# Expert blocks: down-projection weights in two fp32r halves, and two row buffers in place of three

## The reference, cut to what matters

```
def expert_block(args):
    tok, e = args
    xb = h_pad[tok]                                     # 128 gathered rows of 1024
    a = jax.nn.silu(xb @ w_gate[e]) * (xb @ w_up[e])    # 128 x 256
    return a @ w_down[e]                                # 128 x 1024
```

## Time and profile before

| what | value |
|---|---|
| median of 3 runs | 3767.45 us (3759.51 to 3767.55) |
| profiled execution, its time | 3764.93 us |
| its span | 3763.1 us |
| PE busy | 3462.2 us, 92% |
| DVE busy | 2725.4 us, 72% |
| ACT busy | 1236.3 us, 33% |
| POOL busy | 485.1 us, 13% |
| the two expert sections | from about 2012 to 2673 us, and 3047 to 3700 us |

### The profile page before, as it was taken

One profiled execution on the slowest core, in us unless ns is written; L12 is line 12 of the kernel. 1 busy time (PEld: TensorE's weight loads), 2 busy tenths in 40 slices (PEclk: granted clock), 3 DMA queues, 4 the chain that ended last, 5 costly groups with the idle time before them and its releaser, 6 DMA issues.

```text
span 3763.1 us, 51806 instructions
## 1 busy us (share of the span) xinstructions
PE 3462.2 (92%) x20788; PEld 2831.3 (75%) x20788; DVE 2725.4 (72%) x3133; ACT 1236.3 (33%) x1641; POOL 485.1 (13%) x465
## 2 busy tenths in 40 slices
PE   8998999999997999998889999999679789999995
PEld 8996798999984788996546776776567666776774
DVE  8877577879877577876667777777464677777774
ACT  1013111000024211011324565565221345655652
POOL 0000220101001210101001121221010011211210
PEclk9999989999998899999989999999899999999998
DMA  6545333454544333541026999999632269999993
GB/s 242 185 161 198 116 134 125 179 190 180 195 160 155 135 124 137 188 157 67 23 90 239 377 364 360 362 359 369 242 123 101 78 223 337 343 343 332 344 333 127
DMA packets 118803, 799.30 MB, mean 212 GB/s; under 512 B 33808, under 2 KB 34832, under 8 KB 48400
## 3 DMA queue, kind: packets, MB, share of 16 engines
q1 hardware_dynamic: 78480, 735.14, 52.6%
q0 software_dynamic: 39024, 59.61, 4.7%
q10 hardware_dynamic: 1040, 1.05, 0.1%
HBM read 808.77 MB, written 71.83 MB: 234 GB/s over the span
## 4 chain that ended last, share of the span: by engine, by line
PE 56%; DVE 9%; ACT 3%; issue 1%; DMA 1%; POOL 0%; DVEq 0%; ACTq 0%; SPq 0%; POOLq 0%
PE ps L433 52%; PE ps L447 4%; DVE ring_r L391 1%; DMA arena<-yd_dram 1%; DVE ring_r L390 1%; DVE arena L2050 1%; ACT arena L1689 0%; ACT arena L1871 0%; DMA ring<-stream_dram 0%; DVE ring_r L2557 0%; DVE arena L1855 0%; DVE mrow L1853 0%; ACT arena L1824 0%; ACT arena L1866 0%; DVE arena_r L516 0%
## 5 line engine op out<-in xcount | busy, mean ns | idle before, releaser
L433 PE MATMUL ps<-arena_r,ring_r 128*128 128x256 f32 (+1 forms) x9968 | 1301.6, 290 | 57.7 <-DVE ring_r L391 26.1
L433 PEld LDWEIGHTS ps<-arena_r,ring_r 128*128 128x128 f32 x9968 | 1249.8, 191 | 95.0 <-DVE ring_r L391 26.9
L433 PE MATMUL ps<-ring_r,arena_r 128*128 128x512 f32 (+1 forms) x2440 | 664.0, 388 | 6.0 <-DVE arena_r L1922 5.1
L433 PEld LDWEIGHTS ps<-ring_r,arena_r 128*128 128x128 f32 x2440 | 442.8, 189 | 97.2 <-DVE arena_r L1922 5.5
L433 PE MATMUL ps<-ring,arena 128*128 128x512 f32 (+1 forms) x1224 | 491.0, 544 | 1.0 <-DVE arena L2592 1.0
L391 DVE TENSOR_TENSOR ring_r<-ring,ring_r 128x4096 fp32r<-128x4096 f32 (+2 forms) x111 | 483.2, 4353 | 3.8
L2557 DVE TENSOR_TENSOR ring_r<-ring,arena_hi 128x2048 fp32r<-128x2048 f32 x154 | 353.1, 2293 | 98.8 <-ACT arena_hi L2602 88.1
L433 PE MATMUL ps<-arena_hi,arena_r 128*128 128x512 f32 x1232 | 406.4, 397 | 0.0
L433 PEld LDWEIGHTS ps<-ring,arena 128*128 128x128 f32 x1224 | 220.3, 192 | 197.5 <-issue 185.2
L433 PE MATMUL ps<-arena 128*128 128x128 f32 (+5 forms) x1728 | 252.4, 326 | 88.5 <-DMA arena<-yd_dram 32.7
L390 DVE CAST ring_r<-ring 128x4096 fp32r<-128x4096 f32 (+2 forms) x111 | 275.8, 2485 | 69.9 <-PE ps L433 57.5
(11 more groups left out here) (322 smaller groups left out, 3079.3 us busy)
## 6 DMA issues: line engine op xcount, KB each, us to landing
ring<-wexp_dram SPq DMA_DIRECT2D x387, 1024.0 KB
ring<-stream_dram SPq DMA_DIRECT2D x143, 2048.0 KB, 7.8
arena<-yd_dram SPq DMA_DIRECT2D x12, 2048.0 KB, 10.4
xd_dram<-arena POOLq DMA_DIRECT2D x6, 512.0 KB, 5.9
consts_sb<-consts_dram SPq DMA_DIRECT2D x1, 2242.0 KB, 16.1
arena<-xd_dram,small POOLq DMA_INDIRECT x129, 8.9
yd_dram<-arena,small POOLq DMA_INDIRECT x129, 8.2
arena<-mem_dram POOLq DMA_DIRECT2D x2, 1024.0 KB, 5.3
```

Source lines behind the costliest of these rows:

```text
L433: return pe.e.matmul(ps, lhsT=lhsT, rhs=rhs, start=start, stop=stop, skip_group_check=True)
```

## The change

The down weights of a block are handled as the gate and up weights are. ACT casts each 512-column half of them to a high half (`act_high_down`, two casts per block, behind silu); POOL, not DVE, subtracts for the low half (`low_down`, two subtractions per block), in place in the ring. `down` on PE becomes 12 fp32r matmuls. DVE now leaves two buffers for the hidden values, the cast `ATH` and the low half `ATL`. The room for the new high halves (three places of 1024 columns, `down_at`) comes from the third row buffer and from one of the five places of "a" and "b", which now rotate through four. POOL fetches three blocks ahead instead of four.

```diff
@@ places
-        for i, o in enumerate((4096, 6144, 8192 + 4096)):
+        for i, o in enumerate((4096, 6144, 8192 + 4096, 8192 + 10240)):
...
-        XB = [sub(8192 + 1024 * i, 1024) for i in range(3)]
+        XB = [sub(8192 + 1024 * i, 1024) for i in range(2)]
...
-                self.hi_at = [rings_r[:, 2048 * (NRAW + i):2048 * (NRAW + i) + 2048] for i in range(10 - NRAW)] + [h[:, :] for h in hi_parts]
+                self.hi_at = [rings_r[:, 2048 * (NRAW + i):2048 * (NRAW + i) + 2048] for i in range(10 - NRAW)] + [h[:, :] for h in hi_parts[:2]]
+                self.down_at = [hi_parts[2][:, 0:1024], hi_parts[2][:, 1024:2048], hi_parts[3][:, :]]
...
+            def raw_down(self, i, nn, of=rings):
+                return v3(self.raw("d", i, of), 1024)[:, :, 512 * nn:512 * nn + 512]
@@ pe_section, down
-                wd = S.raw("d", i)
+                ah, al = as_r(ATH.v()), as_r(ATL.v())
                 for nn in range(2):
                     ps = take(pe, K, "y", i, nn)
                     for k in range(2):
-                        o = 1024 * k + 512 * nn
+                        wh, wl = S.hi_down(i, nn)[:, k, :], S.raw_down(i, nn, rings_r)[:, k, :]
                         pe.wait_ge(*at("left", K, "h", i))
-                        pe.wait_ge(*S.got("d", i))
-                        ins = mm(pe, ps[:, :], AT.v(128 * k, 128), wd[:, o:o + 512], k == 0, k == 1)
+                        pe.wait_ge(*at(K, "split down", i, nn))
+                        mm(pe, ps[:, :], ah[:, col(k)], wh, k == 0, False)
+                        mm(pe, ps[:, :], ah[:, col(k)], wl, False, False)
+                        ins = mm(pe, ps[:, :], al[:, col(k)], wh, False, k == 1)
@@ dve_section
-                    dve.next.tensor_copy(AT.v(0, 256), bank(K, "h", i)[:, 0:256]).then_inc(*dve.mark("left", K, "h", i))
+                    ah, al = as_r(ATH.v()), as_r(ATL.v())
+                    dve.next.tensor_copy(ah, bank(K, "h", i)[:, 0:256]).then_inc(*dve.mark())
+                    dve.next.tensor_tensor(al, bank(K, "h", i)[:, 0:256], ah.bitcast(F32), ALU.subtract).then_inc(*dve.mark("left", K, "h", i))
@@ act_section
+        def act_high_down(act, S, i, nn):
+            act.wait_ge(*S.got("d", i))
+            old = 2 * i + nn - len(S.down_at)
+            if old >= 0:
+                act.wait_ge(*at("ps", S.key, "y", old // 2, old % 2))
+            act.next.copy(S.hi_down(i, nn), S.raw_down(i, nn)).then_inc(*act.mark(S.key, "high down", i, nn))
...
                     act.next.activation(SUM.v(0, 256), bank(K, "hidden", i)[:, 0:256], ACT.Silu, bias=0.0, scale=1.0).then_inc(*act.mark(K, "silu", i))
+                    act_high_down(act, S, i, 0)
+                    act_high_down(act, S, i, 1)
@@ pool_section
+            def low_down(i, nn):
+                pool.wait_ge(*at(K, "high down", i, nn))
+                pool.next.tensor_tensor(S.raw_down(i, nn, rings_r), S.raw_down(i, nn), S.hi_down(i, nn).bitcast(F32),
+                                        ALU.subtract).then_inc(*pool.mark(K, "split down", i, nn))
-            for i in range(min(4, n)):
+            for i in range(min(3, n)):
                 fetch(i)
             for i in range(n + 1):
-                if i + 1 < n and i + 4 < n:
-                    fetch(i + 4)
+                if i + 3 < n:
+                    fetch(i + 3)
+                if i < n:
+                    low_down(i, 0)
                 if i:
                     put(i - 1)
+                if i < n:
+                    low_down(i, 1)
```

More of the change, by code:

```diff
@@ L271, in build @@
         hi_parts = []
-        for i, o in enumerate((4096, 6144, 8192 + 4096)):
-            hi_parts.append(nc.alloc_sbuf_tensor_at(f"arena_hi{i}", [128, 2048], F32R, offset=arena_at + 4 * o))
+        for i, o in enumerate((4096, 6144, 8192 + 4096, 8192 + 10240)):
+            hi_parts.append(nc.alloc_sbuf_tensor_at(f"arena_hi{i}", [128, 2048 if i < 3 else 1024], F32R, offset=arena_at + 4 * o))
         out_parts = []
@@ L290, in build @@
                               [semaphore(f"sec_weights_{i}_{l}_{b0}") for i in range(NRAW)],
-                              [semaphore(f"sec_x_{i}_{l}_{b0}") for i in range(3)],
+                              [semaphore(f"sec_x_{i}_{l}_{b0}") for i in range(2)],
                               [semaphore(f"sec_y_{i}_{l}_{b0}") for i in range(2)])
@@ L2219, in build @@
         XH = [sub(6144 + 1024 * i, 1024) for i in range(2)]
-        SUM, AT = sub(15360, 512), sub(15872, 256)
+        SUM, ATH, ATL = sub(15360, 256), sub(15872, 256), sub(16128, 256)
         OH = [sub(512 * i, 512) for i in range(4)]
@@ L2467, in hi, with hi_down @@
                 return self.hi_at[(2 * i + (part == "b")) % len(self.hi_at)]
+            def raw_down(self, i, nn, of=rings):
+                return v3(self.raw("d", i, of), 1024)[:, :, 512 * nn:512 * nn + 512]
+            def hi_down(self, i, nn):
+                return v3(self.down_at[(2 * i + nn) % len(self.down_at)], 512)
             def got(self, part, i):
@@ L2474, in got_x @@
             def got_x(self, i):
-                return self.x[i % 3], 16 * (i // 3 + 1)
+                return self.x[i % 2], 16 * (i // 2 + 1)
             def put_y(self, i):
@@ L2489, in all_done @@
                     eng.wait_ge(*self.got(*it))
-                for i in range(max(0, self.n - 3), self.n):
+                for i in range(max(0, self.n - 2), self.n):
                     eng.wait_ge(*self.got_x(i))
@@ L2504, in turn @@
                         pe.wait_ge(*S.got_x(i))
-                        ins = tr(pe, ps[:, col(j)], XB[i % 3].v(512 * g + 128 * j, 128))
+                        ins = tr(pe, ps[:, col(j)], XB[i % 2].v(512 * g + 128 * j, 128))
                     ins.then_inc(*pe.mark("ps", K, "x", i, g))
@@ L2640, in fetch @@
             def fetch(i):
-                if i >= 3:
-                    pool.wait_ge(*at("ps", K, "x", i - 3, 1))
+                if i >= 2:
+                    pool.wait_ge(*at("ps", K, "x", i - 2, 1))
                 pool.e.indirect_dma_start(
-                    out=XB[i % 3].v(), out_offset=None, in_=xd,
+                    out=XB[i % 2].v(), out_offset=None, in_=xd,
                     in_offset=bass.IndirectOffsetOnAxis(ap=TOKEN_OF[:, S.b0 + i:S.b0 + i + 1], axis=0),
-                    bounds_check=128 * nt - 1, oob_is_err=False).then_inc(S.x[i % 3], 16)
+                    bounds_check=128 * nt - 1, oob_is_err=False).then_inc(S.x[i % 2], 16)
             def put(i):
```

## The result

| | before | after |
|---|---|---|
| time, median | 3767.5 us (3759.51 to 3767.56, 4 runs) | 3811.74 us (3811.39 to 3817.31, 4 runs) |
| ratio, 95% interval | | 1.013 (1.0116 to 1.0143) |
| profiled execution, time and span | 3764.93, 3763.1 us | 3811.55, 3809.7 us |
| one block, both sections | 10.07 us | 10.41 us in a regular turn |
| first to last output copy, sections 1 and 2 | 637.8, 627.8 us | 663.6, 654.4 us |

The kernel became 1.3% slower, 44 us by the medians, where the forecast of 3842 us had 77 us of loss. The direction and the mechanism came out, the size did not: a block takes 0.34 us longer than before, not 0.57. This block time is the round that POOL and DVE go through together.

What follows compares the result with a forecast made beforehand. PE was taken to bound the kernel, with transfers close behind. Ring 71 us, section ends 4 and starts 2 gave 77 us on the profiled 3764.93 us, so 3842 us; range 3765 to 3900.

Steps and rivals of the forecast that it cites:

- PE: Down on PE takes 2.83 us instead of 3.43, saving 0.60 us a block; PE alone would need 9.47 us.
- ACT and DVE's small parts: ACT's two casts, 2.2 us, fit in 2.45 us before the output copy; DVE's added subtraction, priced at 0.42, costs nothing.
- Room: Fewer row buffers and high places cost nothing in between; a gather is still issued almost two turns (20 us) ahead.
- The meeting: POOL's and DVE's subtractions with two SBUF operands do not run together; one stands still until the other is done.
- The signs that the forecast named: PE below 95%, DVE's subtractions 3.4 then 2.29 us, POOL's first 2.4 to 3.6, pitch near 10.6, transfers near 0.93.
- The ring: POOL's two subtractions, scatter and DVE's pair make a 10.64 us round, 0.57 above 10.07; 125 turns, 71 us.
- The missed turn: Rival: POOL's second subtraction is ready after 4.85 us, DVE goes first; 1.5 us more per block, 3960 us, chance 0.08.
- The ends: The last block of a section waits for both POOL subtractions: 1.9 us more per section, 4 us in all.
- the sections' starts: The third gather waits for the first block's transposes: 0 to 2 us per section, 1 taken, so 2 us.
- The transfers: Transfers limit a block to some 9.77 us (9.87 and 9.67 by layer), cutting off about half of PE's gain.
- the likeliest case: The forecast's own case, the ring of POOL and DVE: 3842 us, own range 3790 to 3885, chance 0.74.
- the first rival: No meeting of POOL and DVE: PE's gain arrives and transfers take over at 9.77 us, 3733 us, chance 0.12.

Runs made afterwards that it cites:

- e3_no_low: Changed kernel without POOL's two subtractions, the product with the low half using the high half again: 3706.33 us.
- e4_room: Kernel before with only the room taken away (two row buffers, gathers three blocks ahead, four high places): 3765.4 us, ratio 1.000.
- e2_memset: Changed kernel with POOL's subtractions replaced by memsets of about 2.5 us each, high half used in place of low: 3719.05 us.
- e6_copy: Changed kernel with each POOL subtraction replaced by two one-operand in-place copies, high half in place of low: 3748.41 us.
- e5_half: Changed kernel with halves for the first 512 down columns only, the other 512 plain float32 matmuls: 3724.7 us, ratio 0.9891.
- e8_three_of_four: Changed kernel with three of four 128 x 512 down-weight pieces in halves, the fourth plain float32: 3721.64 us, ratio 0.988.
- e1: Changed kernel with POOL's order changed, both subtractions of a block before the scatter: 3806.59 us, ratio 1.0112.
- e7: Changed kernel with the second subtraction of a block moved from POOL to DVE, before DVE's weight subtractions: 3752.73 us, ratio 0.9967.

## Why the prediction was right in kind and wrong in size

**PE.** Right. Down now takes twelve matmuls at a pitch of 0.229 us, 2.75 us (2.83 forecast), and without the low half a block of the second section takes 9.47 us (e3_no_low), the forecast's sum.

**ACT and DVE's small parts.** Right: the two casts of the down weights (2.19 us in the block shown) lie in front of the output copy, and neither they nor DVE's added subtraction are on the chain. ACT's share of the chain is its casts of rows and gate and up weights, which now lie inside the round.

**Room.** Right: it costs nothing (e4_room).

**The meeting.** Right. It is exclusion of POOL's reads of SBUF by DVE's two-operand subtraction and the reverse: DVE's instruction goes back to 2.29 us when POOL writes only (e2_memset), is late behind a one-operand copy (e6_copy), and is untouched where the slot suffices (e5_half, e8_three_of_four). The gather that begins inside the pair is held too: it takes 2.89 us and ends 0.9 us behind the first instruction of the pair; DVE's second instruction is not held by it. The signs that the forecast named came as well: PE at 92% of the stretches, the first of DVE's pair at 3.24 us, POOL's first subtraction at 3.5 to 3.6; only the pitch, 10.41, is below its 10.6.

**The ring.** This is the term that was mis-sized, not its form. Forecast: 2.22 + 0.31 + 1.01 + 0.2 + 2.36 + 4.54 = 10.64. Measured: 2.25 + 0.14 + 1.00 + 0.03 + 2.41 + 4.55 = 10.38. In order: POOL's first subtraction, a gap, the scatter, a gap, the second subtraction, DVE's pair. The four durations were right to 0.05 us each; the two gaps were 0.17 us too long each. I had taken the gap in front of the scatter from scatter to gather, a gap between two indirect DMAs, and put it where arithmetic comes before the DMA. In the timeline of after, DMA behind arithmetic waits 0.14 us, and arithmetic behind a DMA 0.03 us. As the ring is only as bad as it exceeds 10.07, an error of 2% in it was one of 40% in the loss: (10.64 - 10.41) x 125 = 29 us, beside the 30 us by which the forecast missed; the other errors nearly cancel (see "The account").

**The missed turn.** The forecast left this out: I had it as a rival, for every block. It came once in each section, here in the first:

```profile
2590.91 3.12 POOL L2672 DMA_INDIRECT yd_dram<-arena,small  x1 [2.56 <-ACT arena_hi L2614]
2594.07 3.70 POOL L2679 TENSOR_TENSOR ring_r<-ring,arena_hi 128x1024 fp32r<-128x1024 f32 x1
```

The scatter began 2.56 us late, inside DVE's next pair (2590.86 to 2595.55), and was held by the pair's first instruction. POOL's second subtraction was then held to the end of the pair and ended at 2597.77; the products behind it followed late, and DVE's next pair came at 2605.06 instead of 2601.3. The turn behind it was 0.7 us shorter, so 3.1 us were lost in the two; in the second section (scatter 2.57 us late at 3653.40) 4.0 us. The round then closed again as before, for DVE had been waiting for PE meanwhile. I had looked for a steady state there and not for a single event. What made the scatter late is open, and no run was made for it. But it is no accident: in all ten traces, in both sections of each, the late one is the 114th indirect DMA of the section. In the kernel before that is a gather, 2.14 us late at no cost; in the kernel after the same count falls on a scatter, with POOL's second subtraction behind it. It made a long turn in the kernel after, e2_memset (11.47 us), e6_copy (13.74 and 14.18) and e8_three_of_four, and none in e1, e3, e4, e5 and e7. Counting the DMAs up to the late one in the trace of before, and then in the new order, would have put one missed turn per section into the forecast.

**The ends.** From the start of the last but one down to the last output copy it takes 9.50 us (2679.04 to 2688.54) and took 8.07: 1.4 us a section, 1.9 forecast. (The forecast's last step is off by itself: 8.05 us and half of the matmuls, 6 x 0.236, make 9.5 and not the 9.7 that it gives.) Of the 1 us at a section's start I found nothing.

**The account.** Ring 0.34 x 125 = 43 us, one missed turn a section 7, ends 3: 53. The forecast had 71, 0, 4 and 2 for the sections' starts. So the ring was 29 us too high and the ends and starts 3, while the missed turns, which it left out, took 7 of that back. The two sections grew by 25.8 + 26.6 = 52.4 us. The profiled execution grew by 46.6; the rest is ahead of and between the sections, where this execution came 7 us earlier to its first hidden product (2005.37 against 2012.38). The other traces, whose code is the same up to there, come at 2008.30 to 2014.69 (e6_copy and e5_half), so most of those 7 us is scatter between executions and no gain. The 6 us between 52.4 and 46.6 are the rest of the miss: 29 + 3 - 7 + 6 = 31, and that the ring's 29 alone nearly equals it is chance.

**The transfers.** Their floor of 9.77 us decided nothing in the likeliest case, but it priced the first rival. e3_no_low shows it 0.11 us too high in the first section (9.87 against 9.76) and 0.2 us too high or more in the second. The step that failed is the scaling of a rate by its busy share.

## What to carry to other kernels

Where two engines exclude each other, their busy shares do not show whether work fits: POOL had 80% of its time free before, with the added work it had about 7 us to do in a block of 10, and yet it made DVE wait in nearly every block. Write down the round of the two engines, all of it, with the DMAs that the same engine issues, and compare the sum with the pace. What matters is the slot left between two turns of the other engine (here 4.79 us). Work cut to fit that slot held DVE up by no more than 0.1 us; the last piece, 1.1 us of POOL's time that no longer fitted, made the block 0.7 us longer (9.7 us in e8_three_of_four, 10.41 with the whole change). Here three quarters of the change gain 1.2% and the whole loses 1.3%. Take the gaps of such a sum from a pair of instructions of the same two kinds; if the trace has none, give the gap its full width in the range. And when one instruction of a trace comes late, count which one it is before calling it an accident.

## What the runs showed of the hardware that was not expected

- A DVE subtraction with two operands in SBUF holds indirect DMAs that POOL issues. They take 2.89 us instead of 1.0 in the kernel after, and in e1_scatter_last 2.87 and 2.11 us; the second of these ends 0.9 us behind DVE's instruction (2343.84 against 2342.94). I had one such row and did not draw from it that the queue can't be rearranged around it.
- The gap on POOL depends on the kinds: 0.31 us from indirect DMA to indirect DMA, 0.14 to 0.16 from arithmetic to DMA and 0.03 from DMA to arithmetic (the kernel after).
- Transfers at a busy share of 0.98 and 366 GB/s went on to 384 to 388 GB/s at 0.99 to 1.00 when the kernel asked for more (e2, e3 and e8, 2100 to 2200 us); between 2300 and 2400 us the same runs have 368 to 370 GB/s at 0.97 to 0.99.
- The 114th indirect DMA of a section begins late, by 2.1 us before and 2.6 after, in both sections of every trace; in e1_scatter_last by about 1 us. Cause open.
